# Sums of squares of single tiles as two rounded matmuls over a high and a low part, and a new order of lifts, splits and the rotary key

## The reference

```
h = RMSNorm(x);  p = h @ W_in
A: differential attention  (aq, ak, av, gate ag): RMSNorm of every 64 of q and k, partial rotary,
   w = softmax(s0) - lam * softmax(s1);  o = RMSNorm_128(w @ v) * (1 - lambda_init)     <- "sub-norm"
B: grouped-query attention (bq, bk, bv, bg): RMSNorm of 128, axial rotary
C: latent attention        (cq 384, ckv 256, ckr 64, cg): RMSNorm of the latents, up-projections to
   qn, qr, kn, v; RMSNorm of qn, kn (128) and of qr, kr (64); rotary on qr and the shared key kr
D: pooling mixer           (du, dg): centred mean windows 2/4/8/16 minus the token, 128x128 matmul
x = x + concat(A, B, C, D each times SiLU(its gate)) @ W_out
```

## Time and profile before

| | us |
|---|---|
| median of 3 runs | 924.63 |
| fastest, slowest of them | 924.15, 1456.06 |
| the profiled execution | 924.1 |
| its span, first to last instruction | 922.3 |
| PE busy, DVE busy, ACT busy | 904.1, 636.8, 585.9 |

### The profile page before, as it was taken

How to read it: one execution, slowest core, us unless ns; L and a number is a source line. 1 busy time by engine, 2 the same in 40 slices (tenths; PEclk the granted TensorE clock), 3 DMA queues, 4 the chain that set the end, 5 groups by cost and what they waited for, 6 DMA issues and landing times.

```text
span 922.3 us, 18111 instructions
## 1 busy us (share of the span) xinstructions
PE 904.1 (98%) x7054; PEld 861.0 (93%) x7054; DVE 636.8 (69%) x1071; ACT 585.9 (64%) x1045; POOL 0.2 (0%) x4
## 2 busy tenths in 40 slices
PE   8989999999999999999999999999999999999998
PEld 7988998998989999999999989999989998999998
DVE  7785897768777776576665658876687667666552
ACT  7677766677666666655554678566686666665331
POOL 0000000000000000000000000000000000000000
PEclk9999999999999999999999999999999999999999
DMA  8644333342334343345444444334425434435552
GB/s 329 256 163 158 137 138 128 138 134 106 140 138 140 138 157 113 138 174 192 165 174 178 181 144 177 125 108 172 146 94 182 136 139 162 150 122 190 201 190 85
DMA packets 22997, 143.83 MB, mean 156 GB/s; under 512 B 2560, under 2 KB 4736, under 8 KB 6528
## 3 DMA queue, kind: packets, MB, share of 16 engines
q1 hardware_dynamic: 22768, 142.64, 43.2%
q10 hardware_dynamic: 144, 0.04, 0.0%
HBM read 140.57 MB, written 2.10 MB: 155 GB/s over the span
## 4 chain that ended last, share of the span: by engine, by line
PE 75%; ACT 11%; DVE 10%; issue 2%; DMA 1%; SPq 0%; ACTq 0%; DVEq 0%
PE dense L721 21%; PE dense L723 21%; PE dense L722 21%; DVE w_lo L1315 4%; ACT w_hi L1010 4%; PE s_ps L885 4%; PE o_ps L920 3%; PE t_ps L901 1%; PE norm_ps L841 1%; ACT y_hi L1139 1%; ACT c_st L1150 1%; DMA raw<-w_stream_dram 1%; ACT c_st L1149 1%; ACT c_st L1151 1%; ACT row L1035 1%
## 5 line engine op out<-in xcount | busy, mean ns | idle before, releaser
L721 PE MATMUL dense<-h_hi,w_hi 128*128 128x272 f32 (+1 forms) x1440 | 427.7, 297 | 4.2 <-ACT row L1035 2.9
L723 PE MATMUL dense<-h_hi,w_lo 128*128 128x272 f32 (+1 forms) x1440 | 413.3, 287 | 0.0
L722 PE MATMUL dense<-h_lo,w_hi 128*128 128x272 f32 (+1 forms) x1440 | 411.5, 286 | 0.0
L1315 DVE TENSOR_TENSOR w_lo<-raw,w_hi 128x1024 fp32r<-128x1024 f32 (+1 forms) x257 | 313.3, 1219 | 104.7 <-ACT w_hi L1010 98.3
L1010 ACT ACTIVATE w_hi<-raw 128x1024 fp32r<-128x1024 f32 (+1 forms) x257 | 271.3, 1056 | 63.6 <-PE dense L723 51.2
L721 PEld LDWEIGHTS dense<-h_hi,w_hi 128*128 128x128 f32 x1440 | 271.3, 188 | 11.2 <-issue 6.7
L722 PEld LDWEIGHTS dense<-h_lo,w_hi 128*128 128x128 f32 x1440 | 271.6, 189 | 1.3
L723 PEld LDWEIGHTS dense<-h_hi,w_lo 128*128 128x128 f32 x1440 | 271.0, 188 | 0.0
L721 PE MATMUL dense<-y_hi,w_hi 128*128 128x272 f32 (+1 forms) x500 | 144.0, 288 | 5.8 <-ACT q_st L1055 2.2
L723 PE MATMUL dense<-y_hi,w_lo 128*128 128x272 f32 (+1 forms) x500 | 142.7, 285 | 0.0
L722 PE MATMUL dense<-y_lo,w_hi 128*128 128x272 f32 (+1 forms) x500 | 142.4, 285 | 0.0
(11 more groups left out here) (161 smaller groups left out, 838.7 us busy)
## 6 DMA issues: line engine op xcount, KB each, us to landing
raw<-w_stream_dram SPq DMA_DIRECT2D x128, 1024.0 KB, 4.8
out_dram<-x SPq DMA_DIRECT2D x8, 256.0 KB, 6.6
x<-xt_dram SPq DMA_DIRECT2D x3, 544.0 KB, 9.2
raw<-w_stream_dram SPq DMA_DIRECT2D x3, 512.0 KB, 7.7
con<-consts_dram SPq DMA_DIRECT2D x1, 984.0 KB, 7.4
x<-xt_dram SPq DMA_DIRECT2D x2, 272.0 KB, 4.8
raw<-w_stream_dram SPq DMA_DIRECT2D x2, 256.0 KB, 4.4
d_w<-consts_dram SPq DMA_DIRECT2D x2, 256.0 KB, 5.1
```

Of the source, the lines that this page charges most:

```text
L721: nc.tensor.matmul(ps, whi, xhi, start=first, stop=False)
L722: nc.tensor.matmul(ps, whi, xlo, start=False, stop=False)
L723: return nc.tensor.matmul(ps, wlo, xhi, start=False, stop=last)
L1315: signal(nc.vector.tensor_tensor(w_lo[:, g % RING, 0:n], raw[:, e % RAW, CHUNK * half:CHUNK * half + n], w_hi[:, g % RING, 0:n].bitcast(F3 ...
```

## The change

For the 30 sums over single tiles (aq, ak, qr, kr, and the sub-norm) the squares are rounded to a high part `sq_hi` by ACT, the low part `sq_lo` is the difference, made by DVE in a new stage `sq_low`, and PE makes two rounded matmuls in place of one float32 matmul. The tables of ones are rounded once at the start (`sums_of`). PE now waits for `summed`, which `sq_low` raises. In the diff, the links and the signal are in `rope_pre` on ACT, and `sub_pre` gains the same last instruction; `sq_low` is on DVE; the copy of the tables is in ACT's stage of the lambdas.

```diff
+        def two(ps, table, hi, lo):
+            nc.tensor.matmul(ps, table, hi, start=True, stop=False)
+            return nc.tensor.matmul(ps, table, lo, start=False, stop=True)
         def rope_stat(l, key, i):
             t0 = rope_from(l, key)
+            pe.wait_ge(summed, sum_no[("rope", l, key, i)])
+            norm_free("rope_stat", l, key, i)
+            half = parity("rope_stat", l, key, i)
             if key in PAIRED:
-                pe.wait_ge(summed, sum_no[("rope", l, key, i)])
+                sums = nc.tensor.matmul(norm_ps[:, t0:L], halves, sq[:, 2 * half, t0:L], start=True, stop=True)
             else:
-                pe.wait_ge(pre_done, pre_no[("rope_pre", l, key, i)])
...
+                sums = two(norm_ps[:, t0:L], halves_r, sq_hi[:, half, t0:L], sq_lo[:, half, t0:L])
         def sub_stat(l, n):
-            pe.wait_ge(pre_done, pre_no[("sub_pre", l, n)])
+            pe.wait_ge(summed, sum_no[("sub", l, n)])
...
+            two(norm_ps[:, t0:L], ones_r, sq_hi[:, half, t0:L], sq_lo[:, half, t0:L]).then_inc(stat_done, 1)
...
+            link(nc.scalar.activation(sq[:, 2 * half, t0:L], src, ACT.Square))
+            link(nc.scalar.activation(qw[:, half, t0:L], src, ACT.Copy, scale=pcol(l, key)))
+            signal(nc.scalar.activation(sq_hi[:, half, t0:L], sq[:, 2 * half, t0:L], ACT.Copy),
+                   pre_done, pre_no[("rope_pre", l, key, i)])
...
+        def sq_low(what, *of):
...
+            dve.wait_ge(pre_done, pre_no[(("rope_pre" if what == "rope" else "sub_pre"), *of)])
+            half = parity(*stage)
+            signal(nc.vector.tensor_tensor(sq_lo[:, half, t0:L], sq[:, 2 * half, t0:L],
+                                           sq_hi[:, half, t0:L].bitcast(F32), ALU.subtract), summed,
+                   sum_no[(what, *of)])
...
+            nc.scalar.activation(sums_of[:, :], con[:, CC["ones"]:CC["ones"] + 256], ACT.Copy).then_inc(ones_ready, 1)
```

```diff
-GATE_LATER = {("cg", 0): 5, ("cg", 1): 4, ...
+GATE_LATER = {("cg", 0): 5, ("cg", 1): 6, ...
+MOVED = {**{("lift", l, 3, 0): -0.55 for l in range(DEPTH)},
...
-        at(s + 4, ("rope_pre", l, "kr", 0, None))
-        at(s + 5, ("rope_stat", l, "kr", 0))
-        at(s + 6, ("rope_fin", l, "kr", 0))
+        at(s + 8, ("rope_pre", l, "kr", 0, None))
+        at(s + 8, ("sq_low", "rope", l, "kr", 0))
+        at(s + 9, ("rope_stat", l, "kr", 0))
+        at(s + 10, ("rope_fin", l, "kr", 0))
```

```diff
-    def tile_from(l, kind):
-        return first_query(l) if kind in ("aq", "bq", "ag", "bg", "cg", "dg") else 0
+    def tile_from(l, kind, j=0):
+        if kind == "du":
+            return first_query(l) // 2
+        return first_query(l) if kind in ("aq", "bq", "cq", "ag", "bg", "cg", "dg") or (kind, j) == ("cqr", 0) else 0
```

More of the change, by code:

```diff
@@ L141, in at @@
     def at(slot, stage):
-        kind = "y_gate" if stage[:2] == ("y_split", "gate") else stage[0]
+        kind = {"gate": "y_gate", "lat_fin": "y_lat"}.get(stage[1], "y_split") if stage[0] == "y_split" else stage[0]
         if kind in at_engine:
@@ L175, in make_plan @@
                     at(s, ("rope_pre", l, kind, i0 + j, j))
+                    at(s, ("sq_low", "rope", l, kind, i0 + j))
                     at(s, ("rope_stat", l, kind, i0 + j))
@@ L236, in make_plan @@
                 at(s, ("sub_pre", l, n))
+                at(s, ("sq_low", "sub", l, n))
                 at(s, ("sub_stat", l, n))
@@ L288, in build @@
     sq = sb("sq", [128, 4, L])
+    sums_of = sb("sums_of", [128, 256], F32R)
+    sq_hi = sb("sq_hi", [128, 2, L], F32R)
+    sq_lo = sb("sq_lo", [128, 2, L], F32R)
     qw = sb("qw", [128, 2, L])
@@ L302, in build @@
     lam_in = v_st[:, 0, 0:DEPTH * 256]
[L303 to L307, removed]
+    lam_sum = v_st[:, 1, 0:DEPTH * 2]
+    neg_lam, eps_c, one_c = stat[:, 2:2 + DEPTH], stat[:, 6:7], stat[:, 7:8]
     dense = [bank("dense0"), bank("dense1")]
@@ L570, in tile_place @@
             return row[:, j, 8 + tile_from(l, kind):8 + L]
-        return c_st[:, {"cq": j, "ckv": 3 + j, "cqr": (2, 5)[j]}[kind], :]
+        return c_st[:, {"cq": j, "ckv": 3 + j, "cqr": (2, 5)[j]}[kind], tile_from(l, kind, j):L]
     gates_of_layer = len(gate_no) // DEPTH
@@ L835, in rope_stat @@
             t0 = rope_from(l, key)
+            pe.wait_ge(summed, sum_no[("rope", l, key, i)])
+            norm_free("rope_stat", l, key, i)
+            half = parity("rope_stat", l, key, i)
             if key in PAIRED:
[L837 removed]
+                sums = nc.tensor.matmul(norm_ps[:, t0:L], halves, sq[:, 2 * half, t0:L], start=True, stop=True)
             else:
[L839 to L842 removed]
+                if (l, key) == (0, "kr"):
+                    pe.wait_ge(ones_ready, 1)
+                sums = two(norm_ps[:, t0:L], halves_r, sq_hi[:, half, t0:L], sq_lo[:, half, t0:L])
             sums.then_inc(stat_done, 1)
@@ L924, in sub_stat @@
         def sub_stat(l, n):
-            pe.wait_ge(pre_done, pre_no[("sub_pre", l, n)])
+            pe.wait_ge(summed, sum_no[("sub", l, n)])
             norm_free("sub_stat", l, n)
             t0 = first_query(l)
-            nc.tensor.matmul(norm_ps[:, t0:L], ones, sq[:, 2 * parity("sub_stat", l, n), t0:L],
-                             start=True, stop=True).then_inc(stat_done, 1)
+            half = parity("sub_stat", l, n)
+            two(norm_ps[:, t0:L], ones_r, sq_hi[:, half, t0:L], sq_lo[:, half, t0:L]).then_inc(stat_done, 1)
         run = dict(setup=warm_up, chunk=chunk, xsum=xsum, rope_stat=rope_stat, lat_stat=lat_stat, v_turn=v_turn, mix=mix,
@@ L1034, in lift @@
                         act.wait_ge(gate_done, gate_no[("gate", prev[0], pk, i, j)])
-            signal(nc.scalar.activation(tile_place(l, p, j), ps[:, 0:L - tile_from(l, kind)], ACT.Copy), lifted,
+            signal(nc.scalar.activation(tile_place(l, p, j), ps[:, 0:L - tile_from(l, kind, j)], ACT.Copy), lifted,
                    scaled_no[(l, p, j)])
@@ L1100, in sub_pre @@
             buffers_free("sub_stat", l, n)
-            signal(nc.scalar.activation(sq[:, 2 * parity("sub_stat", l, n), t0:L], o_ps[:, t0:L], ACT.Square), pre_done,
+            half = parity("sub_stat", l, n)
+            link(nc.scalar.activation(sq[:, 2 * half, t0:L], o_ps[:, t0:L], ACT.Square))
+            signal(nc.scalar.activation(sq_hi[:, half, t0:L], sq[:, 2 * half, t0:L], ACT.Copy), pre_done,
                    pre_no[("sub_pre", l, n)])
```

58 lines of the change are left out of this document (29 added, 29 removed).

## The result

The changed kernel takes **930.1 us** (median of four runs, 929.0 to 930.8) against 924.6 for the kernel before run beside it: a ratio of 1.006, 95% interval 1.004 to 1.008. Slower by 0.6%, where 920 was forecast with a range of 908 to 928. The profiled execution took 930.8 us, span 929.0.

What follows compares the result with a forecast made beforehand. TensorE, busy 98% of the span, was taken to bound the kernel. -5.9 - 1.9 - 8.3 + 1.6 + 10.5 = -4.0 took 924.1 to 920 us, range 908 to 928 (the forecast's own range 915 to 924).

Steps and rivals of the forecast that it cites:

- Part 5: At the 30 rounded sums, PE waits in order for the DVE's subtraction: 10.5 us more, bounds 0 and 20.
- Part 1: Single-tile sums on PE: two rounded matmuls, 0.25 us, replace a float32 sum of 0.46; 5.9 us less over 30.
- Part 2: Second layer: fewer columns in cq, the first tile of cqr and du; 1.9 us less, bounds 0 and 2.5.
- Parts 3 and 4: PE's PSUM bank waits: reordered lifts save 8.3 us; kr's new place delays a lift, 1.6 us more.
- v_st's 1.6: PE's wait for v_st: called untouched, as kr's three ACT instructions take the place of a gate's three.
- The late lift near 90 us: Lift of cg's third tile, after kr's new place: 1.0 us later, PE waits 0.6 to 1.0 in each layer.
- (b): kr and a y_hi no longer precede the q_st lift: 1.1 us go in the first layer, a like wait in the second.
- ten were read as late: Of 24 aq, ak and sub-norm sums, ten late: seven in the first layer (7.6 us), three in the second (6.6).
- 2.5 for chains: Off the 14.2 us of late sums: a first wait also gives the next late sum its time, 0.9 and 1.6.
- 1.2 for regained time: Off the 14.2 us of late sums: the DVE loses its waits for y_hi, 12.7 us; 1.2 taken off.
- rival B: In-order ak and sub-norm sums make PE wait 18 us: 928, deciding from 14.5 us of waits; chance 0.2.
- the two worst sums: PE's sum waits behind the DVE's split: near 168, 1.8 us late; first sub-norm of the second layer, 2.8 late.

Runs made afterwards that it cites:

- 922.9: Kernel before with only the narrower tiles of the second layer (cq, the first tile of cqr, du): 922.9 us, ratio 0.9986.
- 911.5: Changed kernel with all 30 sums back in float32 and kr's preparation, sum and finish back in their old slots: 911.5 us, ratio 0.986.
- 918.3: Changed kernel with all sums in float32, plus 30 unused rounded copies on ScalarE whose end releases each sum: 918.3 us, ratio 0.994.
- 913.3: Changed kernel with all 30 single-tile sums back in float32, moves and narrower columns kept: 913.3 us, ratio 0.988.
- 926.6: Changed kernel with 20, 22 and 16 extra matmuls in PE's three longest waits for the low part: 926.6 us in nine runs.
- three equal pauses of 3.05: Kernel before with six PE pauses made by idle ScalarE copies, the last three 3.05 us each: 951.0 us, ratio 1.029.
- the last kernel: Moves and narrower columns, only ten of 30 sums rounded, kr in its old slots: 910.8 us, ratio 0.9855.

## Why the prediction was wrong

It failed at **Part 5**, which had the mechanism right and its size wrong, and by a term it did not have, the clock.

- Part 1 (-5.9): right where it can be seen. The pair costs 0.25, and chunks that hold a rounded sum nobody waits for gain 0.2 each. No run measures the 5.9 of all thirty by itself.
- Part 2 (-1.9): right as a saving, 1.2 in time.
- Parts 3 and 4 (-8.3 + 1.6): from 922.9 to 911.5 the moves without kr's give 11.4, and kr's costs 1.8: -9.6 where -6.7 was forecast. Which of the other moves gives how much was not tested. One wait that the prediction called untouched, v_st's 1.6, goes with them and comes back to half with kr's. The late lift near 90 us is there (0.94 from start to start, and 1.46 at the same place of the second layer). (b) was half right: kr did hold the lift that the third tile of the up-projection waits for, but a wait of 0.6 came back at the fifth.
- Part 5 (+10.5): **+19.2**. Of it 5.0 are the copies (918.3 less 913.3). The other 14.2 are what is left for the subtraction: 926.6 less 918.3, with the 5.9 of the rounded passes added back. PE's waits say the same in another way: 17.4 at the sums, less 0.3 there in the float32 kernel, and 0.9 more than there for v_st and 1.0 for row, make 19.0. Three things were mis-sized. The copies: the prediction laid 13 us on ScalarE and wrote that this "costs nothing as such", pricing only the places of the sums and not the lifts behind them. The count of late sums: ten were read as late, with 14.2 us, and 13 were, with 17.4. And the deductions, 2.5 for chains and 1.2 for regained time: the chains exist (with the sub-norm's wait gone, ak 2 waited 2.9 in place of 0.65), but what was left out was more than what was taken off. That the 14.2 left for the subtraction equals the 14.2 read in place is chance: the first rests on the 5.9 of Part 1 as forecast, the second on ten late sums where there were 13.
- The clock (0 in the sum): **+3.5**, measured by filling the waits.

-5.9 - 1.2 - 9.6 + 19.2 + 3.5 = +6.0, from 924.1 to 930.1. This adds up by construction, as the terms are the differences of one run and the next, from the kernel before over the columns, the moves and the filled waits to the changed kernel; it is no check of them. Against the forecast of 920 they are 8.7 (Part 5), 3.5 (the clock) and 0.7 (Part 2) too much and 2.9 (Parts 3 and 4) too little: without the moves' unforeseen 2.9, which was luck, the miss would have been 13 us and not 10.

What happened is rival B, whose mark was waits of 14.5 us: they are 15.0. B gave 928; the clock carried the time past the range. The chance of 0.2 for B was too low, as the forecast stood at 10.5 after deductions from 14.2, at the edge of B, and both unpriced items (copies, clock) point the same way. The prediction also named the two worst sums and their cause, the split ahead of the subtraction, rightly; the experiment with the low part ahead of that split confirms it.

Not settled: what ate the 0.8 between the last kernel and the sum of its gains (0.3 of it lies in the traces at the lift near 550 us, where the ten rounded sums gained 0.3 only with kr in its late place); and when exactly a wait of 3 us costs the clock, as equal waits did and did not.

## What to carry to other kernels

An instruction that replaces another must be priced with what produces its operands: here 0.2 us saved on the bounding engine needed 0.43 and 0.44 on two others, in order, between instructions that the bounding engine waits for. For 5.9 us saved, 19.2 came back in waits and 3.5 in clock. Price such helpers by what stands behind them on their own queue, not by the engine's share. And when a change makes TensorE wait for microseconds, look at the granted clock behind the wait: behind the wait of 3.0 us at 167 it cost 2.7 more, and a wait that cannot be removed can be filled.

## What the runs showed of the hardware

- Behind waits of PE of 1.9 to 5.1 us the granted clock fell to half (1.2 of 2.4 GHz) for 3.4 or 6.8 us, but not behind each: a wait of 3.1 us at 680 left it at 1.00, those of 3.0 at 167 and 2.4 at 695 did not, and of three equal pauses of 3.05 two did. The kernel with the low part ahead of the split, whose longest waits are 1.9 us, has full clock in two runs and not in three; in its trace the clock fell 2 us behind the wait that ends at 167.5. Runs of one kernel at different mean clocks differ by up to 3 us. The Trainium skill, "TensorE: Matmul & The Clock Gate", "HAM oscillation — how this bites in real kernels", tells of waits between bursts of matmuls behind which the clock is down again and the next burst starts slow. The trace agrees in kind: the chunk behind the wait at 167 took 7.2 us in place of 4.5. But it did not happen behind every wait.
- DVE and ACT were busy 4.7 and 4.0 of 5 us while PE waited at 167, and the clock still fell; 58 useless matmuls in those waits kept it at 1.00.
